# FFN gate and up of a split-precision transformer kernel: the high weights meet both parts of x in one 512-column product, four PSUM banks per chunk, halves added by VectorE, and gate/up loads issued ahead of down loads

## The reference

```python
def rmsnorm(x, g):
    y = x * lax.rsqrt(jnp.mean(x * x, axis=-1, keepdims=True) + EPS)
    return y * g

def swiglu(h, w_gate, w_up, w_down):          # 1024 x 2816, 1024 x 2816, 2816 x 1024
    return (jax.nn.silu(h @ w_gate) * (h @ w_up)) @ w_down

x = x + 0.5 * swiglu(rmsnorm(x, ffn1_norm[i]), ffn1_w_gate[i], ffn1_w_up[i], ffn1_w_down[i])
...
x = x + 0.5 * swiglu(rmsnorm(x, ffn2_norm[i]), ffn2_w_gate[i], ffn2_w_up[i], ffn2_w_down[i])
```

## Time and profile before

| | before |
|---|---|
| time, median of 3 runs | 2114.8 us (2111.72 to 2115.3) |
| span of the profiled execution | 2110.5 us |
| profiled execution's own time | not given apart from its span; the three runs above lie 1.2 to 4.8 us over it |
| TensorE busy | 1841.2 us (87%) |
| VectorE busy | 802.8 us (38%) |
| ScalarE busy | 598.7 us (28%) |
| mean granted TensorE clock | 0.924 |
| chain that ended last | TensorE 59%, DMA 36%, VectorE 2%, ScalarE 1% |
| DMA over the span | 286 GB/s; about 428 GB/s in the second half of the span |

### The profile page before, as it was taken

One profiled execution on the slowest core, in us unless ns is written; L12 is line 12 of the kernel. 1 busy time (PEld: TensorE's weight loads), 2 busy tenths in 40 slices (PEclk: granted clock), 3 DMA queues, 4 the chain that ended last, 5 costly groups with the idle time before them and its releaser, 6 DMA issues.

```text
span 2110.5 us, 30801 instructions
## 1 busy us (share of the span) xinstructions
PE 1841.2 (87%) x13330; PEld 1364.1 (65%) x13330; DVE 802.8 (38%) x940; ACT 598.7 (28%) x705; POOL 133.3 (6%) x140
## 2 busy tenths in 40 slices
PE   8999999999999999999999986676777677777766
PEld 8999997999999997699999831222223212122221
DVE  6556556655756564766568500000000000000000
ACT  5334546443433355643347300000000000000001
POOL 4100011400000000220002000000000000000000
PEclk9999999999999999999999987898787879788788
DMA  7555552455555554065566999999999999999998
GB/s 260 189 181 170 162 185 98 168 179 179 201 165 194 195 168 145 21 209 180 179 205 210 423 409 427 429 427 428 429 429 428 428 429 429 428 428 428 429 428 347
DMA packets 182536, 603.95 MB, mean 286 GB/s; under 512 B 11952, under 2 KB 139440, under 8 KB 158016
## 3 DMA queue, kind: packets, MB, share of 16 engines
q1 hardware_dynamic: 180560, 601.43, 73.5%
q10 hardware_dynamic: 1648, 0.96, 0.2%
q0 software_dynamic: 256, 0.52, 0.1%
HBM read 601.84 MB, written 1.05 MB: 286 GB/s over the span
## 4 chain that ended last, share of the span: by engine, by line
PE 59%; DMA 36%; DVE 2%; ACT 1%; issue 1%; SPq 0%; ACTq 0%; POOL 0%; DVEq 0%; POOLq 0%
PE ps L1045 21%; DMA bulk<-in_w_up 17%; PE ps L1059 12%; DMA bulk<-in_w_down 8%; DMA bulk<-in_w_gate 8%; PE ps L1222 3%; PE ps L1618 3%; DMA keep<-in_w_up 2%; PE ps L1644 2%; DMA keep<-in_w_down 2%; PE ps L1116 2%; PE ps L1011 2%; PE ps L1115 2%; PE ps L1117 2%; PE ps L1239 1%; PE ps L1577 1%
## 5 line engine op out<-in xcount | busy, mean ns | idle before, releaser
L1045 PE MATMUL ps<-part,part 128*128 128x256 f32 x3840 | 460.2, 280 | 0.4 <-DVE part L2212 0.4
L1045 PEld LDWEIGHTS ps<-part,part 128*128 128x128 f32 x3840 | 455.5, 188 | 1.0 <-DVE part L2212 0.8
L1618 PE MATMUL ps<-bulk 128*32 128x512 f32 x1616 | 255.8, 765 | 150.6 <-DMA bulk<-in_w_up 93.0
L2212 DVE TENSOR_TENSOR part<-bulk,part 128x2048 fp32r<-128x2048 f32 x88 | 202.9, 2347 | 255.5 <-ACT part L1710 255.5
L1618 PEld LDWEIGHTS ps<-bulk 128*32 128x32 f32 x1616 | 50.8, 125 | 339.4 <-issue 135.1
L1059 PE MATMUL ps<-part,part 128*128 128x256 f32 x2112 | 255.5, 280 | 0.0
L1059 PEld LDWEIGHTS ps<-part,part 128*128 128x128 f32 x2112 | 251.8, 188 | 0.2 <-issue 0.2
L1710 ACT ACTIVATE part<-bulk 128x2048 fp32r<-128x2048 f32 x86 | 160.1, 1910 | 258.0 <-DMA bulk<-in_ffn_w_up 243.8
L2785 DVE TENSOR_TENSOR keep<-keep,ps 128x512 f32<-128x512 f32 x16 | 11.0, 687 | 544.0 <-PE ps L1618 544.0
L1644 PE MATMUL ps<-bulk,keep 128*32 128x512 f32 x784 | 109.4, 693 | 23.6 <-DMA bulk<-in_w_down 23.0
L2221 DVE TENSOR_TENSOR part<-bulk,part 128x2048 fp32r<-128x2048 f32 x46 | 105.6, 2311 | 46.0 <-ACT part L1725 46.0
(11 more groups left out here) (309 smaller groups left out, 2229.8 us busy)
## 6 DMA issues: line engine op xcount, KB each, us to landing
bulk<-in_w_gate SPq DMA_DIRECT2D x53, 2048.0 KB, 40.7
bulk<-in_w_up SPq DMA_DIRECT2D x48, 2048.0 KB, 39.7
bulk<-in_w_down SPq DMA_DIRECT2D x48, 2048.0 KB, 40.2
bulk<-in_ffn_w_gate SPq DMA_DIRECT2D x44, 1024.0 KB, 7.5
bulk<-in_ffn_w_up SPq DMA_DIRECT2D x44, 1024.0 KB, 10.0
bulk<-in_ffn_w_down SPq DMA_DIRECT2D x44, 1024.0 KB, 5.2
keep<-in_w_up SPq DMA_DIRECT2D x16, 2048.0 KB, 40.7
keep<-in_w_down SPq DMA_DIRECT2D x15, 2048.0 KB, 40.4
```

Of the source, the lines that this page charges most:

```text
L1045: ins = pe.matmul(y, w_, x_, start=(k == m == 0), stop=(k == KD - 1 and m == 2))
L1618: ins = pe.matmul(ps[j * CAP:(j + 1) * CAP, half, :], xe[:, k, :], w[:, kk, j * HALF:(j + 1) * HALF], start=(k == 0), stop=(k == KD - 1))
L2212: dve.tensor_tensor(hi(slot(3 * b + i)), slot(3 * b + i), as32(w_hi(f, b, i)), ALU.subtract).then_inc(gu_split, 1)
```

## The change

Gate and up are computed with the high weights against both parts of x in one product of 512 columns (`product`): x_high and x_low of a block k are read as one moving operand (`pair`), and the result fills a bank, high part in columns 0:T, low part in T:2T. The low weights with high x (256 columns) are added to T:2T. A chunk now takes 32 products of 512 and 32 of 256 columns, in four banks: gate in 0 and 1, up in 2 and 3, the same for every chunk. ScalarE copies the half T:2T out of PSUM (`low_half`), VectorE adds the half 0:T to it (`gate_sum`, `up_sum`) and multiplies with 1/rms afterwards. Gate of the next chunk waits for `gate_free` (the gate sum), its up for `gu_free` (the up sum). In the first chunk of the first FFN the products stay 96 single ones of 256 columns, into the four banks. The loads of gate and up of chunk c + 1 are issued before the down load of chunk c, and the third FFN's first gate and up are loaded and split within the second FFN's last chunks. What is left out of the diff below: the semaphores' names, the removed `ffn_chunk`, and places where `hi(xnT)` and `hi(xT_lo)` become `x_high` and `x_low`.

```diff
--- before.py
+++ after.py
@@ -203,6 +203,15 @@
 
         def as32(ap):
             return hi(ap).bitcast(F32)
+
+        def pair(first, second):
+
+
+            at, to = [(bulk_at if ap.tensor.name == bulk.name else keep_at) + 4 * ap.offset for ap in (first, second)]
+            k, n = first.shape[1:]
+            low, size = min(at, to), abs(to - at) // 4 + k * n
+            both = nc.alloc_sbuf_tensor_at(f"pair{low}_{size}", [P, size], F32R, offset=low)
+            return bass.AP(both, (at - low) // 4, [[size, P], [n, k], [(to - at) // 4, 2], [1, n]])
 
         zero_bf = ctx.enter_context(nc.sbuf_tensor("zero_bf", [1, HALF], BF16))
 
...
@@ -645,6 +658,9 @@
         xT_lo = v3(6160, KD, T)
         hid_lo = view(8208, 4 * CW).rearrange("p (b j t) -> p b j t", b=2, j=2)
 
+        x_pair = pair(xnT, xT_lo)
+        x_high, x_low = x_pair[:, :, 0, :], x_pair[:, :, 1, :]
+
         PAR = (0, 0, 1, 1)
 
         def w_hi(f, b, i):
...
@@ -782,12 +794,23 @@
                     sp.dma_start(mem_rows, A["mem"][0].rearrange("(t p) d -> p t d", p=P)).then_inc(mem_loaded, 16)
                     dn_load(0, 1, 1 - p)
                 else:
-                    ffn_chunk(f, 0, p)
-                    ffn_chunk(f, 1, 1 - p)
+                    if f != 2:
+                        gu_loads(f, 0, p)
+                        dn_load(f, 0, p)
+                        gu_loads(f, 1, 1 - p)
+                    else:
+                        gu_loads(f, 1, 1 - p)
+                        dn_load(f, 0, p)
+                    dn_load(f, 1, 1 - p)
+                gu_loads(f, 2, p)
                 with sp.Fori(1, N_ODD) as i:
-                    ffn_chunk(f, 2 * i, p)
-                    ffn_chunk(f, 2 * i + 1, 1 - p)
-                ffn_chunk(f, NCH - 1, p)
+                    gu_loads(f, 2 * i + 1, 1 - p)
+                    dn_load(f, 2 * i, p)
+                    gu_loads(f, 2 * i + 2, p)
+                    dn_load(f, 2 * i + 1, 1 - p)
+                if f == 1:
+                    gu_loads(2, 0, PAR[2])
+                dn_load(f, NCH - 1, p)
 
             def mix_loads(n0, n1):
                 for n in range(n0, n1):
@@ -995,21 +1018,33 @@
                 def terms(b, i, j, k):
                     w_l, w_h = [hi(s).rearrange("p (k n) -> p k n", k=KD) for s in (slot(3 * b + i), w_hi(f, b, i))]
                     w_l, w_h = [w[:, k, j * P:(j + 1) * P] for w in (w_l, w_h)]
-                    return (w_h, hi(xnT)[:, k, :]), (w_h, hi(xT_lo)[:, k, :]), (w_l, hi(xnT)[:, k, :])
+                    return (w_h, x_high[:, k, :]), (w_h, x_low[:, k, :]), (w_l, x_high[:, k, :])
+
+                def product(b, i, j, k):
+
+                    (w_h, _), _, (w_l, x_h) = terms(b, i, j, k)
+                    y = bank(2 * i + j)
+                    pe.matmul(y, w_h, x_pair[:, k], start=(k == 0), stop=False, skip_group_check=True)
+                    return pe.matmul(y[:, T:2 * T], w_l, x_h, start=False, stop=(k == KD - 1), skip_group_check=True)
 
                 def gate_up_first(b):
 
                     if f:
                         pe.wait_ge(gu_split, NCH * f * 2 + 2)
-                    for k in range(KD if f else 0):
+                    for k in range(KD - 2 if f else 0):
                         if k % 2 == 0:
                             fed(n, k // 2)
-                        for j in range(2):
-                            for i in range(2):
-                                y = ps[:, 2 * b + j, i * T:(i + 1) * T]
-                                for m, (w_, x_) in enumerate(terms(b, i, j, k)):
-                                    ins = pe.matmul(y, w_, x_, start=(k == i == m == 0), stop=(k == KD - 1 and m == 2),
-                                                    skip_group_check=True)
+                        for i in range(2):
+                            for j in range(2):
+                                product(b, i, j, k)
+                    if f:
+                        fed(n, KD // 2 - 1)
+                        for i in range(2):
+                            for j in range(2):
+                                for k in (KD - 2, KD - 1):
+                                    ins = product(b, i, j, k)
+                            if i == 0:
+                                ins.then_inc(gate_full, 1)
                     for m, i in () if f else ((0, 0), (1, 0), (0, 1), (1, 1), (2, 0), (2, 1)):
                         if m == i == 0:
                             pe.wait_ge(gate0_half, 1)
@@ -1026,26 +1061,24 @@
                                 fed(n, k // 2)
                             for j in range(2):
                                 w_, x_ = terms(b, i, j, k)[m]
-                                ins = pe.matmul(ps[:, 2 * b + j, i * T:(i + 1) * T], w_, x_, start=(k == i == m == 0),
-                                                stop=(k == KD - 1 and m == 2), skip_group_check=True)
+                                ins = pe.matmul(bank(2 * i + j)[:, min(m, 1) * T:(min(m, 1) + 1) * T], w_, x_,
+                                                start=(k == m == 0), stop=(k == KD - 1 and m == 2), skip_group_check=True)
+                        if m == 2 and i == 0:
+                            ins.then_inc(gate_full, 1)
                     ins.then_inc(gu_used, 1)
                     if f:
                         mean_square(n, bank(4)).then_inc(rsum_done, 1)
 
                 def gate_up(c, b, between=None):
-                    if not (isinstance(c, int) and c < 2):
-                        pe.wait_ge(gu_free, NCH * f + c - 1)
-                    for j in range(2):
-                        for i in range(2):
-                            if j == 0:
-                                pe.wait_ge(gu_split, (c + NCH * f) * 2 + i + 1)
-                            y = ps[:, 2 * b + j, i * T:(i + 1) * T]
+                    for i in range(2):
+                        pe.wait_ge((gate_free, gu_free)[i], NCH * f + c)
+                        pe.wait_ge(gu_split, (c + NCH * f) * 2 + i + 1)
+                        for j in range(2):
                             for k in range(KD):
-                                for m, (w_, x_) in enumerate(terms(b, i, j, k)):
-                                    ins = pe.matmul(y, w_, x_, start=(k == m == 0), stop=(k == KD - 1 and m == 2))
-                            if between is not None and i == 0:
-                                between[j]()
-                    ins.then_inc(gu_used, 1)
+                                ins = product(b, i, j, k)
+                            if between is not None and j == 0:
+                                between[i]()
+                        ins.then_inc((gate_full, gu_used)[i], 1)
 
                 def down(c, b, first=False, last=False):
                     pe.wait_ge(dn_split, c + NCH * f + 1)
...
@@ -1738,7 +1771,23 @@
             def ffn(f):
                 p = PAR[f]
                 q = 1 - p
+                def low_half(c, i, dst):
+                    act.wait_ge((gate_full, gu_used)[i], c + NCH * f + 1)
+                    act.activation(dst, ps[:, 2 * i:2 * i + 2, T:2 * T], ACT.Copy).then_inc(low_out, 1)
+
+                def low_halves(c, b):
+
+                    if not (isinstance(c, int) and f == 0 and c < 2):
+                        act.wait_ge(hid_ready, c + NCH * f - 1)
+                    low_half(c, 0, gate_sb[:, b])
+                    if not (isinstance(c, int) and f == c == 0):
+                        act.wait_ge(hid_full, c + NCH * f)
+                    if isinstance(c, int) and c == 0:
+                        act.wait_ge(sum_done, (0, 2, 3, 5)[f] + 1)
+                    low_half(c, 1, up_sb)
+
                 split_gu(f, 1, q)
+                low_halves(0, p)
                 split_dn(f, 0, p)
                 if f == 0:
                     act.wait_ge(const_loaded, 16)
@@ -1754,6 +1803,8 @@
                     act.activation(small[:, 18:20], small[:, 18:20], ACT.Sqrt, bias=epsc, scale=1.0 / D).then_inc(mem_ssq, 1)
 
                 def chunk(c, b, gu=True, dn=True):
+                    if not (isinstance(c, int) and c == 0):
+                        low_halves(c, b)
                     act.wait_ge(ga_done, c + NCH * f + 1)
                     act.activation(gate_sb[:, b], gate_sb[:, b], ACT.Silu).then_inc(gate_done, 1)
                     if isinstance(c, int) and f == c == 0:
@@ -1761,6 +1812,8 @@
                             evac(f"mh{b_}", memhat[:, 2 * b_:2 * b_ + 2, :], tbank(f"mh{b_}"))
                     if gu:
                         split_gu(f, c + 2, b)
+                    elif f == 1 and dn:
+                        split_gu(2, 0, b)
                     if dn:
                         split_dn(f, c + 1, 1 - b)
 
@@ -1772,9 +1825,7 @@
                 chunk(NCH - 3, p)
                 chunk(NCH - 2, q, gu=False)
                 chunk(NCH - 1, p, gu=False, dn=False)
-                if f == 1:
-                    split_gu(2, 0, q)
-                else:
```

(23 more changed lines are left out.)

23 lines of the change are left out of this document (12 added, 11 removed).

## The result

The kernel after takes 2127.32 us (median of 4, 2126.12 to 2128.95) against 2114.19 for the kernel before beside it (median of 4, 2111.72 to 2115.3): a ratio of 1.0066, 95% interval 1.0054 to 1.0079. It is slower by 13 us. The forecast was 2102.5 us, 2088 to 2116.

What follows compares the result with a forecast made beforehand. TensorE's product stream was taken to bound the FFNs, weight transfers the experts behind. A gain of 28.4 us and losses of 16.1 gave -12.3 us, from 2114.8 to 2102.5 us, range 2088 to 2116.

Steps and rivals of the forecast that it cites:

- the gain: Gate and up: a pair of 512 and 256 columns takes 332.8 ns, 0.66 us less per chunk, 28.4 over 43 chunks.
- The rival with a fixed cost: Product stream: 11.1 ns per product whatever its length; gain 15.5 us, losses 16.1, 2115.4 us, no change; chance 0.09.
- The rival that named the missing row: Product stream: no gain from length, pair stays at 353 ns, only losses left, 2131 us; chance 0.03.
- The estimate from the figures of the Trainium skill: Product stream: about 2.5 ns per matmul beside N/2.4; gain 3.4 us in all, new waits win, 2127.5 us.
- Steady state: Some 36 chunks behind the FFN starts: gate sum ready before TensorE needs it, so new waits cost nothing.
- the cover: Steady chunks: gate sum ready after 20.6 us, TensorE there after 21.95; margin 1.3 us at worst, some 3 more likely.
- Starts: Start of each FFN: gate waits for late gate sums at chunks 1 and 2; 3.4 and 1.2, 6.0, 1.2, 3.2 us.
- The sum of the losses: All FFNs: waits at starts, 0.6 for joins and 0.5 for last chunks, 16.1 us together; bounds 8 and 24.
- Slower: Whole kernel: the outcome of a time more than 0.2% (4.2 us) above the kernel before; chance 0.12.

Runs made afterwards that it cites:

- The first run: A kernel of products alone, 96 of each type and length, the rest of the computation left out: fp32r 227.0 ns for 512 columns, 120.0 for 256.

## Why the prediction was wrong

**The step that failed** is in the gain: "So 118 ns is the pace of loading weights, and a long product hides its successor's load." The pair was priced at 332.8 ns and takes 353; 28.4 us of gain are 0.

Both rows under it were of another kind than the product in question, and one was misread. Line 1577's 118 ns for 32 columns is a real floor for short fp32 products (111 ns here for 64 and 128 fp32r columns), but two different things came out near 118: 256 columns of fp32r cost 113 to 127 by the places of their data, and neither a longer product nor, in the kernel's pattern, narrower weights take that away. Line 1394 is plain fp32. Its 8 records are those of 4 products of two passes each, so 3.43/8 = 429 ns is one pass of 512 columns; halving it to 214.5 "per pass" made a stream at half pace look like one at full pace. The first run shows the same: 192 records of 256 columns for 96 products, 216 ns each. So the row said nothing of a long fp32r product.

In the kernel after, such a product is followed by the next start after 233 ns, 20 more than the 213.3 of its columns, and the short one after 121. What three products paid beyond their columns (3 x 11.1 ns) two now pay. The rival with a fixed cost (2115.4) falls for this kernel, as it needs 342 ns a pair; in the first run alone its form fits. Why the cost beyond the columns is shared out so stays open.

The rival that named the missing row, "no row shows an fp32r product of 512 columns, and if one took as long as two of 256 (235.6 ns), the pair would stay at 353 ns", is what happened: 353 ns a pair, and 2127.3 us against its 2131. It was given 0.03 on the strength of the fp32 rows. The estimate from the figures of the Trainium skill (TensorE: Matmul & The Clock Gate, "Wait — 56ns, not 53.3ns?"), 2127.5, lands on the result by luck: it takes 109.2 ns per product of 256, which fp32r never reached.

**Steady state.** Right: cost nothing, no wait of TensorE in the chunks behind the starts. With pairs at 353 the cover was also 0.7 us per gate and up larger than reckoned.

**Starts.** 16.1 us forecast; FFN 1 ends 4.0 us later than before, and the other three take 5.9, 0.3 and 3.2 more from end to end, 13.5 of the 13.7 us by which the spans differ. FFN 1: 3.4 and 1.2 forecast, 3.42 and 1.20 measured as idle time; gate of chunk 1 began 3.0 us later than before, since 0.38 us of idle stood there already. FFN 2: 6.0 is right only as a sum, by luck. "Nothing in the change moves GpSimd's operation" held in the program and not in time: it met the two short operations that now stood there, 4.3 us, and a low clock behind it added 1.5; the wait for the gate sum that was forecast at 6.0 did not come. FFN 3: 1.2 forecast, absorbed, since two pairs' worth of missing gain (2 x 0.66 us) brought TensorE there later than reckoned. FFN 4: 3.2 forecast; 1.79 of waiting, the rest behind it at a low clock. The sum of the losses had no term for the clock.

**Chances.** Slower had 0.12; the mechanism with the missing row should have been weighed against the forecast, not put behind it: the whole gain hung on a duration that no row showed.

## What to carry to other kernels

A gain that hangs on the price of an instruction form is worth nothing until a row shows that form: fp32 rows don't price fp32r, and a pitch near a known floor isn't that floor. A row's count should be held against the products in the program before its time is divided by passes. In this kernel merging two fp32r products with the same weights saved nothing; in bare runs it saved 13 ns in one layout and would have cost 6 in another, so it has to be measured with the kernel's own places. Fewer than 256 columns save little (111 ns for 64 and for 128). A cheaper type in long runs does save. And where two engines' short operations can meet GpSimd's long ones, hold GpSimd back until the critical ones are through.

## What the runs showed of the hardware

fp32r products of 256 columns took 113.3 to 120.0 ns at the full clock with data at multiples of 8 words, and up to 126.6 at odd places, depending on the places of weights and x in memory and on the neighbouring products, against 109.2 for bf16; products of 512 columns took 227 to 233, of 128 and of 64 columns 111. Beyond an estimate of the columns alone that is 7 to 20 ns, in one run the same for 256, 384 and 512 columns, in another three times as much for 512 as for 256. Weights of 64 columns brought 256 columns from 120.0 to 113.5, weights of 32 columns in the kernel's pattern only from 117.8 to 117.3. Changing between fp32r and bf16 inside each group of three cost 6.7 ns per group over fp32r alone, although bf16 by itself is no slower. VectorE's cast and product of 128x512 took 4.58 and 2.40 us beside GpSimd's cast and subtraction of 128x2048, and 0.43 and 0.69 with these held back. In the kernel after the granted clock fell to 0.50 after waits of 4.32 and 1.79 us without products, at a cost of 1.5 and 1.6 us, and did not fall after one of 3.42 us; in other runs it fell during or after waits of 3.46 to 4.70 us at that same place, at a cost of 1.5 to 2.5.
